# Values of mLSTM and retention as three fp32r products of high and low parts, in a kernel of four layers on one core

## The chip, the cores and the metric

One Trainium2 chip, one core. The metric is the device time of one execution in microseconds (us). The kernel before was timed in three runs; one further execution was profiled.

## The reference, cut to what matters

Two blocks of two layers each, on 256 tokens of 1024 features. The change touches the first block's two mixers and one product of the second block:

```python
rq = _rotary(r_q, pos); rk = _rotary(r_k, pos) * 128 ** -0.5          # 4 heads of 128
scores = einsum('bnihd,bnjhd->bnhij', q, k) * decay                   # retention
o = einsum('bnhij,bnjhe->bnihe', scores, v) + ...                     # v: 4 heads of 256
qk = einsum('bnthd,bnshd->bnhts', q, k) * D                           # mLSTM
num = einsum('bnhts,bnshe->bnthe', qk, v) + ...; den = qk.sum(-1) + ...
tail = cumsum(log_keep, axis=3, reverse=True)                         # second block, stick breaking
```

The kernel computes the two chunks of 128 tokens as one causal product over all 256, so that "scores" is three tiles of 128 x 128 per head (384 columns), and values are the products of these tiles with v, the tile as stationary operand. In mLSTM a column of ones beside v gives den.

## The kernel before, in words

**The main stream.** All weights come in units of four k tiles x 512 columns (1 MB). SyncE issues each unit's DMA into one of three `raw` buffers; ScalarE writes its high part (`wh`, fp32 rounded to fp32r, line 947); VectorE subtracts that from raw and writes the low part (`wl`, line 1372); TensorE takes the units in order out of a ring of four. Every projection is three fp32r products: high x high, low x high, high x low. A group (two units, as a rule) is either row-wise ("tok": the activations are stationary, 512 columns of weights stream, output tokens x features) or column-wise ("col": the weights are stationary, 256 tokens stream, output features x tokens). The groups of a first-block layer are mv0, mv1, gate, mqk0, mqk1, rv0, rv1, rq, rk, ga0, ga1, gb0, gb1, rg0, ... (`B1`); those of a second-block layer are q, k, av, ag, cqk, b, cvg, o0, o1.

**PSUM.** Groups take turns on two pairs of banks (`main`, `freed`); TensorE opens both banks of a pair at the start of a group and waits until they have been read. mqk0 has the pair that mv1 had, with the short gate group between. Four other banks (`aux`) serve the small steps, in the order of `AUX1` and `AUX2`.

**The small steps.** `SIDE1` and `SIDE2` say after which pair of k tiles of which group a step is woven in; there are four such slots a group. The engines' programs each walk the same table. "s h" is a head's mLSTM scores, "v h t" its values for token half t, "tq"/"tk" the transposes of rotated q and k, "rs h" and "rp h" scores and values of retention, "sk" the sums of stick breaking. Scores and values are plain fp32 products, which the trace shows as two passes each. VectorE multiplies the scores with the decay in place (line 1510), then TensorE may run the values (line 663). For retention, q and k come out row-wise; VectorE rotates them (lines 1556 to 1561), TensorE transposes (line 670), ScalarE copies to `rqT` and `rkT` (line 1042). ScalarE copies v out of PSUM (`copy_mv`, line 993, `copy_rv`, line 1036) and with that frees v's banks.

In VectorE's program a group first does the low parts that are due, then its slots, then `evac`, what is to be done with the finished banks; lines of one engine run strictly in this order.

## Time and profile before

| | |
|---|---|
| three runs, median (lowest, highest) | 1176.04 us (1175.67, 1177.94) |
| profiled execution, its own time | 1177.04 us |
| its span | 1175.2 us |
| TensorE busy | 1158.7 us, 99% |
| VectorE busy | 747.7 us, 64% |
| ScalarE busy | 570.4 us, 49% |
| DMA, mean over the span | 180 GB/s |
| granted TensorE clock, mean | 0.995 |

Busy time of TensorE counts each matmul until its modelled end, and a matmul begins while the one ahead drains; so the distance from start to start, not the duration, tells what one costs. The time outside of the span (1177.04 - 1175.2) is launch and end.

### The profile page before, as it was taken

What the parts mean: (1) busy time and instruction counts of PE and PEld (TensorE: products, weight loads), DVE (VectorE), ACT (ScalarE), POOL (GpSimd) and SP (SyncE); (2) the same over time, 40 slices, a digit from 0 to 9 for tenths busy, and PEclk for the clock granted to TensorE, in tenths of its full rate; (3) what the DMA queues carried; (4) which work ended last, traced back from release to release, by engine and by line L of the source; (5) the groups of instructions that cost most, each with busy time, mean ns of one, the idle gap of its engine ahead of it and who ended that gap; (6) DMA issues with size and microseconds to landing.
All of it is one profiled execution on the core that took longest, in us unless ns stands there. A gap on an engine that the chain in (4) does not pass through costs nothing.

```text
span 1175.2 us, 18028 instructions
## 1 busy us (share of the span) xinstructions
PE 1158.7 (99%) x7546; PEld 1042.8 (89%) x7546; DVE 747.7 (64%) x1006; ACT 570.4 (49%) x658; POOL 26.2 (2%) x36
## 2 busy tenths in 40 slices
PE   8999999999999999999999999999999899999997
PEld 6988998998999988998998898899988689978996
DVE  4867557667655546686764667755545667875775
ACT  5563445442544434454544534444432466755664
POOL 0000000001000000000000000000000100000000
PEclk9999999999999999999999999999999999999999
DMA  9664454556666463745446556665566353437330
GB/s 340 224 215 144 144 183 176 182 186 199 225 213 191 165 212 115 250 146 177 160 143 200 169 190 215 223 202 183 183 197 215 125 203 124 141 123 263 113 104 36
DMA packets 129871, 211.45 MB, mean 180 GB/s; under 512 B 6528, under 2 KB 52608, under 8 KB 129664
## 3 DMA queue, kind: packets, MB, share of 16 engines
q1 hardware_dynamic: 128048, 204.02, 52.1%
q0 software_dynamic: 1744, 6.29, 1.9%
q8 instruction: 60, 0.98, 0.3%
q14 instruction: 19, 0.16, 0.0%
HBM read 209.24 MB, written 1.05 MB: 179 GB/s over the span
## 4 chain that ended last, share of the span: by engine, by line
PE 92%; DVE 3%; ACT 3%; issue 1%; DMA 0%; POOL 0%; SPq 0%; DVEq 0%; POOLq 0%; ACTq 0%
PE ps L470 88%; PE ps L663 1%; DVE wl L1372 1%; ACT wh L947 1%; PE ps L698 1%; PE ps L603 1%; ACT sg L1110 0%; DMA rv<-in_w_in 0%; PE ps L801 0%; DVE sg L1652 0%; PE ps L670 0%; PE ps L783 0%; DVE xl L1458 0%; ACT xh L983 0%; DVE X L1631 0%
## 5 line engine op out<-in xcount | busy, mean ns | idle before, releaser
L1372 DVE TENSOR_TENSOR wl<-raw,wh 128x2048 fp32r<-128x2048 f32 (+1 forms) x190 | 424.1, 2238 | 175.6 <-ACT wh L947 175.2
L947 ACT ACTIVATE wh<-raw 128x2048 fp32r<-128x2048 f32 (+1 forms) x190 | 359.9, 1900 | 181.7 <-PE ps L470 166.9
L470 PE MATMUL ps<-xh,wh 128*128 128x256 f32 x1200 | 337.3, 282 | 0.0
L470 PE MATMUL ps<-xl,wh 128*128 128x256 f32 x1200 | 332.3, 277 | 0.0
L470 PE MATMUL ps<-xh,wl 128*128 128x256 f32 x1184 | 328.5, 277 | 0.0
L470 PEld LDWEIGHTS ps<-xh,wh 128*128 128x128 f32 x1200 | 225.9, 188 | 3.2 <-issue 2.4
L470 PEld LDWEIGHTS ps<-xl,wh 128*128 128x128 f32 x1200 | 225.9, 188 | 0.4
L470 PEld LDWEIGHTS ps<-xh,wl 128*128 128x128 f32 x1184 | 222.7, 188 | 0.0
L470 PE MATMUL ps<-wh,xh 128*128 128x512 f32 (+1 forms) x512 | 203.9, 398 | 4.9 <-DVE wl L1372 2.7
L470 PE MATMUL ps<-wl,xh 128*128 128x512 f32 (+1 forms) x512 | 197.3, 385 | 0.0
L470 PE MATMUL ps<-wh,xl 128*128 128x512 f32 (+1 forms) x512 | 197.2, 385 | 0.0
L470 PEld LDWEIGHTS ps<-wh,xh 128*128 128x128 f32 x512 | 96.9, 189 | 26.3 <-DVE wl L1372 4.3
L470 PEld LDWEIGHTS ps<-wh,xl 128*128 128x128 f32 x512 | 96.9, 189 | 19.8
L470 PEld LDWEIGHTS ps<-wl,xh 128*128 128x128 f32 x512 | 97.1, 190 | 17.6
L470 PE MATMUL ps<-wh,hdh 128*128 128x512 f32 x176 | 68.7, 390 | 0.0
L470 PE MATMUL ps<-wl,hdh 128*128 128x512 f32 x176 | 68.5, 389 | 0.0
L470 PE MATMUL ps<-wh,hdl 128*128 128x512 f32 x176 | 68.5, 389 | 0.0
L1102 ACT ACTIVATE tmp<-ps 128x512 f32<-128x512 f32 x18 | 10.8, 598 | 63.5 <-PE ps L470 63.5
L470 PEld LDWEIGHTS ps<-wh,hdl 128*128 128x128 f32 x176 | 33.0, 188 | 6.9
L470 PEld LDWEIGHTS ps<-wl,hdh 128*128 128x128 f32 x176 | 33.0, 188 | 6.8
L470 PEld LDWEIGHTS ps<-wh,hdh 128*128 128x128 f32 x176 | 33.0, 188 | 6.6
L425 POOL TENSOR_TENSOR small<-small,cst 128x1 f32<-128x1 f32 (+1 forms) x18 | 17.9, 992 | 894.9 <-DVE small L1660 392.4
(269 smaller groups left out, 1394.5 us busy)
## 6 DMA issues: line engine op xcount, KB each, us to landing
raw<-in_w_in SPq DMA_DIRECT2D x90, 1024.0 KB, 5.0
raw<-in_w_gate_up SPq DMA_DIRECT2D x88, 512.0 KB, 4.8
raw<-in_w_down SPq DMA_DIRECT2D x20, 1024.0 KB, 5.0
raw<-in_w_out SPq DMA_DIRECT2D x16, 1024.0 KB, 5.0
raw<-in_w_proj_ret SPq DMA_DIRECT2D x8, 1024.0 KB, 4.9
raw<-in_w_proj_mlstm SPq DMA_DIRECT2D x8, 1024.0 KB, 4.9
rows<-in_ln_g POOLq DMA_DIRECT2D x4, 512.0 KB, 4.4
rows<-in_ln_b POOLq DMA_DIRECT2D x4, 512.0 KB, 6.0
```

The lines of the kernel that those rows point to most:

```text
L425: pool.tensor_tensor(o, in_, C("mhalf", 0, n), ALU.pow).then_inc(after, 1)
L470: return pe.matmul(o, a, b, start=start, stop=False, skip_group_check=True)
L603: r = pe.transpose(bank[:, tok_half(g)], src[:, P * (4 * q + g):P * (4 * q + g) + P], ident)
L663: r = pe.matmul(bank[:, 0:257], dd_of(h)[:, o:o + P], mv[:, s, h, 0:257], start=(s == 0), stop=(s == t))
L698: r = pe.transpose(bank[:, S * k2 + P * t:S * k2 + P * t + P], src[:, t, tok_half(k)], ident)
L947: act.activation(stretch(wh, u, 0, m), source(u)[:, 0:m], ACT.Copy).then_inc(s_hi, 1)
L1102: act.activation(a_[:, :], main(name, l)[0][:, :], ACT.Silu).then_inc(freed_by(name, l, 0), 1)
L1372: dve.tensor_tensor(stretch(wl, u, a, nk * n), source(u)[:, a:nk * n], f32(stretch(wh, u, a, nk * n)), ALU.subtract).then_inc(s_lo, 1 if a ...
```

## The change

- Values of mLSTM and retention: v is split into `mvh`/`mvl` and `rvh`/`rvl`, decayed scores into `ddh`/`ddl` and `rdh`/`rdl`, all fp32r; each product becomes three (high x high, low x high, high x low). ScalarE writes the high part of v, VectorE the low part, and it is VectorE that now frees v's banks. Scores themselves stay plain fp32. The ones beside v are two columns of `mvh` (258 columns), written once a layer by VectorE.
- rq and rk are column-wise groups. ScalarE copies each bank with its two partition halves exchanged into `tmp` (`swap`), VectorE multiplies with cos and sin tables of 256 columns each (before: 128 each) and adds. The transposes and their copies are gone, and with them four entries of `AUX1`.
- The stick-breaking sums multiply `below` with 384 columns at once, not 256 and 128.
- The first load of the LRU gate weights `gw` moves from the start of POOL's program to behind the first block's last norm, the second to a later event; `gw` lies in the shared area. New buffers are laid over old areas with pads.

```diff
-for _name, _n in (("ident", 128), ("dec", 1024), ("cc", 128), ("ss", 128), ("negm", 256), ("negs", 384), ("lnc", 384),
+for _name, _n in (("ident", 128), ("dec", 1024), ("cosr", 256), ("sinr", 256), ("negm", 256), ("negs", 384), ("lnc", 384),
...
-    put("cc", lay(np.cos(ang)))
-    put("ss", lay(np.sin(ang)))
+    put("cosr", np.concatenate([np.cos(ang).T, np.cos(ang).T]))
+    put("sinr", np.concatenate([-np.sin(ang).T, np.sin(ang).T]))
...
-            cols(w, c0, 512, SKEW if c0 in (3072, 3584, 6152, 6664, 7176, 7688) else 0)
+            cols(w, c0, 512, SKEW if c0 in (3072, 3584, 0, 512, 6152, 6664, 7176, 7688) else 0)
...
-        "tq0", "tq1", "tk0", "tk1", "rs0", "rs1", "rp0", "rs2", "rp1", "rs3", "rp2", "rp3",
+        "rs0", "rs1", "rp0", "rs2", "rp1", "rs3", "rp2", "rp3",
...
-    "rk": (("v 3 0",), ("v 3 1",), ("hm1", "tq 0"), ("tq 1", "hm2")),
-    "ga0": ((), (), ("tk 0",), ("tk 1",)),
+    "rk": (("v 3 0",), ("v 3 1",), ("hm1",), ("hm2",)),
...
-            pool.dma_start(gw[:, :, :], A["gw"][0:4].rearrange("n p c -> p n c")).then_inc(s_gw, 16)
...
+            pool.wait_ge(s_xn, 16)
+            pool.dma_start(gw[:, :, :], A["gw"][0:4].rearrange("n p c -> p n c")).then_inc(s_gw, 16)
...
-                    r = pe.matmul(bank[:, 0:257], dd_of(h)[:, o:o + P], mv[:, s, h, 0:257], start=(s == 0), stop=(s == t))
-                r.then_inc(fill, 1)
-
-            def ret_turn(l, which, t):
-                bank, fill = open_aux(f"t{which}{t}", l)
-                pe.wait_ge(s_rot, 4 * l + 2 * (which == "k") + t + 1)
-                for h in range(4):
-                    r = pe.transpose(bank[:, tok_half(h)], tmp[3 + t][:, tok_half(h)], ident)
+                    mm(bank[:, 0:258], ddh[:, h, o:o + P], mvh[:, s, h, :], s == 0)
+                    mm(bank[:, 0:258], ddl[:, h, o:o + P], mvh[:, s, h, :], False)
+                    r = mm(bank[:, 0:DV], ddh[:, h, o:o + P], mvl[:, s, h, :], False)
...
-                    aux_done("tk1", l)
+                    pe.wait_ge(s_rot, 4 * l + 4)
...
+                hi, lo, cols = rdh[h % 2], rdl[h % 2], slice(DV * h, DV * h + DV)
                 for t in range(2):
                     for s in range(t + 1):
                         o = P * t if s == 0 else S
-                        r = mm(bank[:, DV * t:DV * t + DV], tmp[3 + h % 2][:, o:o + P], rv[:, s, DV * h:DV * h + DV], t == 0)
+                        out_ = bank[:, DV * t:DV * t + DV]
+                        mm(out_, hi[:, o:o + P], rvh[:, s, cols], t == 0)
+                        mm(out_, lo[:, o:o + P], rvh[:, s, cols], False)
+                        r = mm(out_, hi[:, o:o + P], rvl[:, s, cols], False)
...
-                for name in ("rv0", "rv1", "rq"):
+                for name in ("rv0", "rv1"):
                     one(name, xh, xl, xw, "tok")
-                one("rk", xh, xl, xw, "tok")
-                for name in ("ga0", "ga1", "gb0", "gb1"):
+                for name in ("rq", "rk", "ga0", "ga1", "gb0", "gb1"):
...
-                        mm(bank[:, 0:S], below[:, :], part[:, h, 0:S], part is eeh)
-                        r = mm(bank[:, S:S + P], below[:, :], part[:, h, S:S + P], False)
+                        mm(bank[:, 0:S + P], below[:, :], part[:, h, :], part is eeh)
...
-                act.activation(mv[:, t, 2 * c:2 * c + 2, 0:256], main(f"mv{c}", l)[t][:, :].rearrange("p (h d) -> p h d", h=2),
-                               ACT.Copy).then_inc(freed_by(f"mv{c}", l, t), 1)
+                act.activation(mvh[:, t, 2 * c:2 * c + 2, 0:DV], main(f"mv{c}", l)[t][:, :].rearrange("p (h d) -> p h d", h=2),
+                               ACT.Copy).then_inc(s_mvh, 1)
...
+                    act.activation(rvh[:, t, col_half(c)], main(f"rv{c}", l)[t][:, :], ACT.Copy).then_inc(s_rvh, 1)
+
+            def swap(l, which):
+                main_full("r" + which, l)
+                for b in range(2):
+                    bank = main("r" + which, l)[b]
+                    if which == "k":
+                        act.wait_ge(s_rot, 4 * l + b + 1)
+                    act.activation(tmp[3 + b][0:64, :], bank[64:P, :], ACT.Copy)
+                    act.activation(tmp[3 + b][64:P, :], bank[0:64, :], ACT.Copy).then_inc(s_swap, 1)
...
+            def mv_low(l, t, c):
+                dve.wait_ge(s_mvh, 4 * l + 2 * c + t + 1)
+                cols = slice(2 * c, 2 * c + 2)
+                dve.tensor_tensor(mvl[:, t, cols, :], main(f"mv{c}", l)[t][:, :].rearrange("p (h d) -> p h d", h=2),
+                                  f32(mvh[:, t, cols, 0:DV]), ALU.subtract).then_inc(freed_by(f"mv{c}", l, t), 1)
+
+            def rv_low(l, c):
+                if c == 0:
+                    dve.wait_ge(s_cst, 16)
+                    dve.tensor_scalar(mvh[:, :, :, DV:DV + 2], C("ident", 0, 16).rearrange("p (t h c) -> p t h c", t=2, h=H), 0.0, 1.0, ALU.mult, ALU.add)
+                for t in range(2):
+                    dve.wait_ge(s_rvh, 4 * l + 2 * c + t + 1)
+                    dve.tensor_tensor(rvl[:, t, col_half(c)], main(f"rv{c}", l)[t][:, :], f32(rvh[:, t, col_half(c)]),
+                                      ALU.subtract).then_inc(freed_by(f"rv{c}", l, t), 1)
+
             def ml_scores(l, h):
                 bank, drained = aux_full(f"s{h}", l)
                 dve.wait_ge(s_dec, 4 * l + h + 1)
-                dve.scalar_tensor_tensor(out=dd_of(h), in0=bank[:, 0:384], scalar=128.0 ** -0.5, in1=dd_of(h), op0=ALU.mult,
-                                         op1=ALU.mult).then_inc(drained, 1)
+                dd, hi = dd_of(h), ddh[:, h, 0:384]
+                after(own(dve.scalar_tensor_tensor(out=dd, in0=bank[:, 0:384], scalar=128.0 ** -0.5, in1=dd, op0=ALU.mult, op1=ALU.mult)))
+                after(own(dve.tensor_copy(hi, dd)))
+                dve.tensor_tensor(ddl[:, h, :], dd, f32(hi), ALU.subtract).then_inc(drained, 1)
...
+                name, dst = "r" + which, rqT if which == "q" else rkT
+                cos, sin = (C(n).unsqueeze(1).broadcast_to([P, 2, S]) for n in ("cosr", "sinr"))
+                for b in range(2):
+                    o, other = dst[:, 2 * b:2 * b + 2, :], tmp[3 + b][:, :].rearrange("p (h t) -> p h t", h=2)
+                    dve.wait_ge(s_swap, 4 * l + 2 * (which == "k") + b + 1)
+                    dve.tensor_tensor(o, main(name, l)[b][:, :].rearrange("p (h t) -> p h t", h=2), cos, ALU.mult).then_inc(freed_by(name, l, b), 1)
+                    after(own(dve.tensor_tensor(other, other, sin, ALU.mult)))
+                    main_done(name, l, b)
+                    dve.tensor_tensor(o, o, other, ALU.add).then_inc(s_rot, 1)
 
             def ret_scores(l, h):
                 bank, drained = aux_full(f"rs{h}", l)
-                dd, dec = tmp[3 + h % 2], C("dec", S * h, S * h + S)
+                dd, dec, hi = tmp[3 + h % 2][:, 0:384], C("dec", S * h, S * h + S), rdh[h % 2][:, 0:384]
                 dve.tensor_tensor(dd[:, 0:S], bank[:, 0:S], dec, ALU.mult)
-                dve.tensor_tensor(dd[:, S:S + P], bank[:, S:S + P], dec[:, 0:P], ALU.mult).then_inc(drained, 1)
+                after(own(dve.tensor_tensor(dd[:, S:S + P], bank[:, S:S + P], dec[:, 0:P], ALU.mult)))
+                after(own(dve.tensor_copy(hi, dd)))
+                dve.tensor_tensor(rdl[h % 2][:, 0:384], dd, f32(hi), ALU.subtract).then_inc(drained, 1)
...
-                dve.memset(mv[:, :, :, 256:258], 1.0)
                 if l == 0:
-                    one("mv0", None, 5)
-                    one("mv1")
+                    one("mv0", lambda: [mv_low(l, t, 0) for t in range(2)], 5)
+                    one("mv1", lambda: [mv_low(l, t, 1) for t in range(2)])
                     before_layers()
                 else:
-                    pair(nothing, nothing, l, lambda: split_x("xb", 0, 1, 2), nothing, nothing)
+                    pair(lambda t: mv_low(l, t, 0), lambda t: mv_low(l, t, 1), l, lambda: split_x("xb", 0, 1, 2), nothing, nothing)
```

VectorE's program from the last units of mv0 to the gate of layer 0, before (wl: low part of a unit; the row wh<-raw,wh of 64x8 is the gate's unit; hb and small: small operations for later):

```order
L1372 TENSOR_TENSOR wl<-hret,wh 128x1024
L1372 TENSOR_TENSOR wl<-raw,wh 128x2048 x2
L1370 TENSOR_TENSOR wh<-raw,wh 128x64x8
L1372 TENSOR_TENSOR wl<-raw,wh 128x2048 x2
L1752 TENSOR_SCALAR hb<-par 128x32
```

and now (mvl: low part of v):

```order
L1385 TENSOR_TENSOR wl<-hret,wh 128x1024 x2
L1385 TENSOR_TENSOR wl<-raw,wh 128x2048 x2
L1383 TENSOR_TENSOR wh<-raw,wh 128x64x8
L1523 TENSOR_TENSOR mvl<-ps,mvh 128x512 x2
L1385 TENSOR_TENSOR wl<-raw,wh 128x2048 x2
L1523 TENSOR_TENSOR mvl<-ps,mvh 128x512 x2
L1773 TENSOR_SCALAR hb<-par 128x32
```

The two mvl of mv1 stand behind the low parts of two units, and ahead of the small operations; the two of mv0 stand behind the gate's unit.

VectorE's program around the first mLSTM scores of layer 0, before (hret holds the decayed scores, BN_STATS reads a finished v(h,t)):

```order
L1372 TENSOR_TENSOR wl<-raw,wh 128x2048 x2
L1510 SCALAR_TENSOR_TENSOR hret<-ps,hret 128x384 x2
L1516 BN_STATS small<-ps 128x6
L1372 TENSOR_TENSOR wl<-raw,wh 128x2048
L1516 BN_STATS small<-ps 128x6
```

and now:

```order
L1385 TENSOR_TENSOR wl<-raw,wh 128x2048
L1529 TENSOR_SCALAR mvh<-cst 128x8x2
L1532 TENSOR_TENSOR rvl<-ps,rvh 128x512 x2
L1385 TENSOR_TENSOR wl<-raw,wh 128x2048
L1539 SCALAR_TENSOR_TENSOR hret<-ps,hret 128x384
L1540 CAST ddh<-hret 128x384
L1541 TENSOR_TENSOR ddl<-hret,ddh 128x384
L1539 SCALAR_TENSOR_TENSOR hret<-ps,hret 128x384
L1540 CAST ddh<-hret 128x384
L1541 TENSOR_TENSOR ddl<-hret,ddh 128x384
L1546 BN_STATS small<-ps 128x6
```

Behind each multiplication with the decay there is a cast and a subtraction; the ones and the low part of rv0 come ahead of the low part of a unit that the scores stood behind already.

## Rows read from the trace of the kernel before

**Rows 1.** The page, part 1, TensorE: busy us, share of the span, instructions.

```profile
PE 1158.7 (99%) x7546; PEld 1042.8 (89%) x7546; DVE 747.7 (64%) x1006; ACT 570.4 (49%) x658; POOL 26.2 (2%) x36
```

**Rows 2.** What TensorE waited for: us in total, times, longest us.

```profile
PE ps L603 <- DVE sg L1652: 3.9, 3, 1.7
PE ps L470 <- DVE wl L1372: 2.7, 2, 2.0
```

**Rows 3.** Busy time of each engine in stretches, TensorE clock, DMA share, GB/s.

```profile
core 0: us, PE busy (x) PEld busy (x) DVE busy (x) ACT busy (x) POOL busy (x), PEclk, DMA share, GB/s
223.00:253.00 30.00, 30.00 (x257) 30.00 (x256) 18.70 (x16) 12.88 (x9) 0.00 (x0) 1.00 0.54 176
310.00:340.00 30.00, 30.00 (x267) 30.00 (x266) 16.73 (x13) 14.08 (x13) 0.00 (x0) 1.00 0.66 208
10.70:14.20 3.50, 3.50 (x9) 2.73 (x10) 3.40 (x4) 2.11 (x2) 0.00 (x0) 0.51 1.06 399
928.90:932.40 3.50, 3.46 (x10) 2.58 (x11) 3.35 (x4) 1.16 (x2) 0.57 (x1) 0.51 0.58 131
1044.90:1048.30 3.40, 3.37 (x18) 2.74 (x19) 2.55 (x5) 2.70 (x3) 0.00 (x0) 1.00 0.22 84
```

**Rows 4.** Timeline, TensorE, first v(h,1): start us, us, engine, line, op, out<-in, count.

```profile
82.69 1.03 PE L663 MATMUL ps<-mv,hret 128*128 128x257 f32 x4
...
83.78 0.39 PE L470 MATMUL ps<-wl,xh 128*128 128x512 f32 x1
```

**Rows 5.** Timeline, TensorE, values of retention of the third head, layer 0.

```profile
142.51 1.46 PE L470 MATMUL ps<-rv,tmp 128*128 128x256 f32 x6
...
143.92 0.28 PE L470 MATMUL ps<-xl,wh 128*128 128x256 f32 x1
```

**Rows 6.** Timeline, TensorE, second transposes of q, layer 0.

```profile
111.10 0.60 PE L670 MATMUL ps<-cst,tmp 128*128 128x128 f32 x4
...
111.66 0.29 PE L470 MATMUL ps<-xl,wh 128*128 128x256 f32 x1
```

**Rows 7.** Timeline, TensorE, sums with below, second block, layer 0.

```profile
1015.44 0.39 PE L470 MATMUL ps<-eeh,below 128*128 128x256 f32 x2
1015.67 0.40 PE L470 MATMUL ps<-eel,below 128*128 128x256 f32 x2
```

**Rows 8.** Timeline, ScalarE, end of mv1, layer 0.

```profile
30.19 1.92 ACT L947 ACTIVATE wh<-raw 128x2048 fp32r<-128x2048 f32 x1 [2.32 <-DMA raw<-in_w_in]
32.02 1.06 ACT L993 ACTIVATE mv<-ps 128x512 f32<-128x512 f32 x2
```

**Rows 9.** Timeline, TensorE, first product of mqk0, layer 0.

```profile
33.33 0.28 PE L470 MATMUL ps<-xh,wh 128*128 128x256 f32 x1
```

**Rows 10.** Timeline, VectorE, same place.

```profile
32.22 2.29 DVE L1372 TENSOR_TENSOR wl<-raw,wh 128x2048 fp32r<-128x2048 f32 x1 [1.95 <-ACT wh L947]
34.43 0.17 DVE L1752 TENSOR_SCALAR hb<-par 128x32 f32<-128x32 f32 x1
```

**Rows 11.** Timeline, VectorE, end of rk, layer 0.

```profile
112.02 0.69 DVE L1556 TENSOR_TENSOR tmp<-ps,cst 128x512 f32<-128x512 f32 x1
...
119.33 2.28 DVE L1372 TENSOR_TENSOR wl<-raw,wh 128x2048 fp32r<-128x2048 f32 x1
```

**Rows 12.** Timeline, VectorE, first scores of mLSTM, layer 0.

```profile
76.57 2.29 DVE L1372 TENSOR_TENSOR wl<-raw,wh 128x2048 fp32r<-128x2048 f32 x1 [4.12 <-ACT wh L947]
78.78 1.22 DVE L1510 SCALAR_TENSOR_TENSOR hret<-ps,hret 128x384 f32<-128x384 f32 x2
```

**Rows 13.** Timeline, TensorE, same place.

```profile
78.59 0.81 PE L470 MATMUL ps<-mqk 128*128 128x256 f32 x4
79.43 0.67 PE L663 MATMUL ps<-mv,hret 128*128 128x257 f32 x2
```

**Rows 14.** Instructions by line and form, VectorE: busy us, mean ns, idle before.

```profile
L1510 DVE SCALAR_TENSOR_TENSOR hret<-ps,hret 128x384 f32<-128x384 f32 x8 | 4.5, 556 | 12.0 <-PE ps L470 11.8
...
L1872 DVE CAST eeh<-ee 128x768 fp32r<-128x768 f32 x4 | 2.2, 560 | 0.1
```

**Rows 15.** Timeline, TensorE, first product of the second unit of ga1.

```profile
129.67 0.28 PE L470 MATMUL ps<-xh,wh 128*128 128x256 f32 x1
```

More of the change, by code:

```diff
@@ L239, in program @@
         ls = sb("ls", [P, 8, 4])
-        gw = sb("gw", [P, 4, P])
         areas = ExitStack()
@@ L255, in program @@
             tmp = [a1(f"tmp{i}", [P, 512]) for i in range(5)]
+        with ExitStack() as areas:
+            sb("pad7", [P, 2048], F32, areas)
+            mvh = sb("mvh", [P, 2, H, 258], F32R, areas)
+            sb("pad8", [P, LINE - 16], F32, areas)
+            ddh = sb("ddh", [P, H, 512], F32R, areas)
+            rvh = sb("rvh", [P, 2, D], F32R, areas)
+            sb("pad9", [P, 2048], F32, areas)
+            ddl = sb("ddl", [P, H, 384], F32R, areas)
+            sb("pad10", [P, 512], F32, areas)
+            mvl = sb("mvl", [P, 2, H, DV], F32R, areas)
+            rvl = sb("rvl", [P, 2, D], F32R, areas)
+            rdh = [sb(f"rdh{i}", [P, 512], F32R, areas) for i in range(2)]
+            sb("pad11", [P, 512], F32, areas)
+            rdl = [sb(f"rdl{i}", [P, 512], F32R, areas) for i in range(2)]
         with ExitStack() as areas:
@@ L284, in program @@
         with ExitStack() as areas:
+            sb("pad6", [P, 14848], F32, areas)
+            gw = sb("gw", [P, 4, P], F32, areas)
+        with ExitStack() as areas:
             sb("pad2", [P, 4096], F32, areas)
@@ L453, in gpsimd @@
                 if l == 1:
-                    _, _, drained, n = aux("2l1", 0)
-                    pool.wait_ge(drained, n + 1)
+                    pool.wait_ge(s_yraw, 2)
                     pool.dma_start(gw[:, :, :], A["gw"][4:8].rearrange("n p c -> p n c")).then_inc(s_gw, 16)
@@ L735, in tensor @@
             }
-            steps["tq"] = lambda l, t: ret_turn(l, "q", t)
-            steps["tk"] = lambda l, t: ret_turn(l, "k", t)
             nothing = lambda: None
@@ L1035, in copy_rv @@
                 for t in range(2):
-                    act.activation(rv[:, t, col_half(c)], main(f"rv{c}", l)[t][:, :], ACT.Copy).then_inc(freed_by(f"rv{c}", l, t), 1)
-            def ret_turn(l, which, t):
-                bank, fill, drained, n = aux(f"t{which}{t}", l)
-                act.wait_ge(fill, n + 1)
-                dst = rqT if which == "q" else rkT
-                act.activation(dst[:, :, tok_half(t)], bank[:, :].rearrange("p (h c) -> p h c", h=4), ACT.Copy).then_inc(drained, 1)
+                    act.activation(rvh[:, t, col_half(c)], main(f"rv{c}", l)[t][:, :], ACT.Copy).then_inc(s_rvh, 1)
[7 more added lines that the diff above has]
+                    act.activation(tmp[3 + b][64:P, :], bank[0:64, :], ACT.Copy).then_inc(s_swap, 1)
             def ret_values(l, h):
@@ L1168, in scalar @@
                     one(f"rv{c}", lambda: copy_rv(l, c))
-                one("rq")
-                one("rk")
+                one("rq", lambda: swap(l, "q"))
+                one("rk", lambda: swap(l, "k"))
                 for n, (dst, o0) in enumerate(((ga, 0), (gb, 8))):
@@ L1541, in rotate @@
             def rotate(l, which):
-                name = "r" + which
-                main_full(name, l)
-                for t in range(2):
-                    bank = main(name, l)[t]
-                    if which == "k":
-                        aux_full(f"tq{t}", l)
-                    if t == 1:
-                        dve.wait_ge(s_rot, 4 * l + 2 * (which == "k") + 1)
-                    x_ = bank[:, :].rearrange("p (h c) -> p h c", c=64)
-                    xs = bank[:, :].rearrange("p (h u c) -> p h u c", u=2, c=64)
-                    cc = C("cc", 64 * t, 64 * t + 64).unsqueeze(1).broadcast_to([P, 8, 64])
-                    ss = C("ss", 64 * t, 64 * t + 64).unsqueeze(1).broadcast_to([P, 4, 64])
-                    a4_ = tmp[2][:, :].rearrange("p (h u c) -> p h u c", u=2, c=64)
-                    b4_ = tmp[3 + t][:, :].rearrange("p (h u c) -> p h u c", u=2, c=64)
-                    dve.tensor_tensor(tmp[2][:, :].rearrange("p (h c) -> p h c", c=64), x_, cc, ALU.mult)
-                    dve.tensor_tensor(b4_[:, :, 0, :], xs[:, :, 1, :], ss, ALU.mult)
-                    dve.tensor_tensor(b4_[:, :, 1, :], xs[:, :, 0, :], ss, ALU.mult).then_inc(freed_by(name, l, t), 1)
-                    main_done(name, l, t)
-                    dve.tensor_tensor(b4_[:, :, 0, :], a4_[:, :, 0, :], b4_[:, :, 0, :], ALU.subtract)
-                    dve.tensor_tensor(b4_[:, :, 1, :], a4_[:, :, 1, :], b4_[:, :, 1, :], ALU.add).then_inc(s_rot, 1)
@@ L1790, in vector @@
                 dve.tensor_scalar(g8, main("gate", l)[0][:, 0:S], R("bif", l), None, ALU.add).then_inc(freed_by("gate", l, 0), 1)
-                for name in ("mqk0", "mqk1", "rv0", "rv1"):
+                for name in ("mqk0", "mqk1"):
                     one(name)
+                for c in range(2):
+                    one(f"rv{c}", lambda: rv_low(l, c))
                 one("rq", lambda: rotate(l, "q"))
```

10 lines of the change are left out of this document (5 added, 5 removed).

## The prediction

> **What bounds the kernel now.** I read the page's table first: TensorE is busy for 99% of the span [rows 1]. Busy time alone proves little, since matmuls overlap, so the next view is the list of TensorE's waits: its two longest entries add up to 6.6 us of 1175 [rows 2]. Then the timeline of the engine: products of high and low parts start one behind the other without a hole, and every step that is woven in between pushes the next product back by its own length. So the kernel takes as long as TensorE's instructions take back to back, plus a few waits. A step that leaves TensorE saves its whole length; an instruction on VectorE or ScalarE costs nothing until TensorE stands waiting for it. The profiled execution took 1177.04 us, its span is 1175.2; the median of the runs shown is 1176.04, so I make the sum in differences and take them from the median.
>
> The unit of the argument: a product of 256 columns in fp32r takes 0.113 us from start to start (267 begin in the 30 us from 310 to 340 [rows 3]), one of 512 twice that, 0.227.
>
> **Part 1, values of mLSTM.** Now v(h,1) is two fp32 products of 257 columns, four passes: the stretch starts at 82.69 and the second normal product behind it at 83.78; less one 0.227 us product that is 0.86 us, so 0.215 us a pass [rows 4]. v(h,0) has half. Per head 1.29 us. After: nine fp32r products of 256 to 258 columns, 9 x 0.114 = 1.03 us. Saved 0.26 us a head, 2.1 us for eight heads.
>
> **Part 2, values of retention.** Six passes run from 142.51 to 143.92, less one product: 1.30 us [rows 5]. After: nine products of 256 columns, 1.02 us. Saved 0.28 x 8 = 2.2 us.
>
> **Part 3, the transposes of q and k.** Four transposes run from 111.10 to 111.66, less one product: 0.45 us [rows 6]. Eight such steps go: 3.6 us. The projections rq and rk keep their columns: 12 products of 256 for a k tile in place of 6 of 512, the same 1.36 us.
>
> **Part 4, one product with below.** A pair of 256 and 128 columns takes 1015.67 - 1015.44 = 0.23 us, as long as two of 256 [rows 7]: the 128 columns pay for 256. As one product of 384 columns at the pace of the long ones it is 0.17. Sixteen pairs: 0.9 us saved. The Trainium skill (TensorE: Matmul & The Clock Gate, section Back-to-back issue gap) speaks against this part: it gives a sustained 81 ns for products of 128 columns with their weight loads, by which the pair would cost 0.19 us, the merging would give about 0.4 us, and the sum would be 0.5 us smaller. The trace disagrees for fp32r.
>
> Parts 1 to 4 take 8.8 us off TensorE.
>
> **What comes back: the hand-over of mv1's banks.** This is the term the diff does not show. After mv1 TensorE has only the gate's short products before mqk0 opens the banks of mv1, both halves at once. Now ScalarE alone frees them: copies at 32.02 for 1.06 us, so until 33.08, and mqk0 starts at 33.33 without a hole [rows 8, 9]. After the change the banks are freed by VectorE's mvl, and in VectorE's order the two mvl stand behind the low part of the next unit, which starts at 32.22 because ScalarE's high part waited for its DMA until 30.19, and is through at 34.43, where the next instruction starts [rows 8, 10]. Two reads of 512 from PSUM follow; one takes 0.69 [rows 11] and two overlapped about 1.30. So the banks are free at 35.7 and mqk0 starts at about 35.8: 2.5 us late. The table of constants grows by 256 columns (128 KB) and the first gw load (256 KB) leaves this stretch: 128 KB at the 399 GB/s of a stretch like it [rows 3] is 0.3 us, by which that DMA lands earlier. I take 2.2 us. Bounds: 0.9 if the mvl were free to run directly behind the copies, 2.9 if the longer table delays the DMA and the missing gw gives nothing. In layer 1 the same four instructions stand in a loose stretch of VectorE; I put 0 there, 0.3 at most. mqk0's late start shifts all that follows by the same amount.
>
> **What comes back: the first value step.** The first decayed scores of a layer are made late: VectorE has the low part that starts at 76.57 ahead of them, the scores start at 78.78, and v(0,0) starts at 79.43, though TensorE was through with the scores' four passes (two of 256, two of 128 columns: 3 x 0.215 = 0.65 us from 78.59) at 79.24 [rows 12, 13]. That wait of 0.19 us is there now. After, the bank is released only behind a cast and a subtraction of 384 columns. The subtraction is like the operation of that size, 0.56 us; the cast lies between 0.56 (768 columns, the row) and the 0.17 of the shortest VectorE operations, I take 0.36 [rows 14, 10]; with two waits of VectorE on itself at some 0.04 it is 1.0 us later. Two layers: 2.0 us, bounds 1.4 and 2.4. The other seven heads have a whole slot, 2.7 us of products and more, between scores and values: nothing there.
>
> **What is hidden.** Rotation: VectorE has six operations of 512 columns for ten shorter ones, about the same time; ScalarE has four half-partition copies more for two fewer, 1.2 us more per projection; low parts of rv, four reads of 0.69 a layer; splits of retention scores, 1.0 us a head. The cover is the ring of four units: the low part that starts at 119.33 (the first of two, so done by 121.6) is for the unit that TensorE enters at 129.67 [rows 11, 15]. Eight microseconds of cover, and no stretch here gains more than three on VectorE. Were it gone, each low part would come late by what exceeds it. On POOL the first gw load moves from the start to behind the first block's last norm; behind it there stand the next gain's load and the powers, which wait for later events, and its reader is the LRU step four groups further on.
>
> **The pace.** Column-wise groups run at one of two paces: 257 products in 30 us from 223 to 253, 267 from 310 to 340 [rows 3], 4% apart, and the pace holds until an insertion changes it. rq and rk become column-wise (384 products of 0.113 us in the two layers), and the insertions that change the pace for them and for the four groups behind (768 products) are other ones. At 4.5 ns a product, half of 1152 being slow is 2.6 us; the four groups pay some 0.8 of it now. Bounds -0.8 (all fast) and +4.4 (all slow). The stretch from 223 to 253 lies behind a direct change from row-wise to column-wise (out of mo1 into yr0), as rq now does behind rv1; but fp32 steps remain that can change it, I take +1.2.
>
> Sum: -8.8 + 2.2 + 2.0 + 1.2 = -3.4; 1176.0 - 3.4 = 1172.6 us.
>
> **Rivals.**
> 1. *The clock falls once more.* TensorE's granted clock fell from 2.4 to 1.2 GHz for some 3.5 us from 10.7, behind the wait of 2.0 us, and from 928.9, behind one of 1.7 us; from 1044.9, behind another of 1.7 us, it stayed whole [rows 2, 3]. The new wait of 2.2 us is of that kind. Half clock for 3.4 us costs 1.7 us: 1174.3 us. For it: the wait is longer than all three. Against: products lie directly ahead of it and behind it.
> 2. *No new waits.* VectorE comes to mvl ahead of the low part, or the split is shorter than I think, and TensorE keeps the whole gain: 1176.0 - 8.8 + 1.2 = 1168.4 us. Against it is the order of VectorE's instructions, which is fixed.
> 3. *The slow pace everywhere.* All 1152 products at the slower pace: 3.2 us more, 1175.8 us. For it: direct changes begin slow.
> 4. *Slower than before: splits stand behind the products.* If the split of each head is ready only when its values step has been reached, 14 more steps wait 1.0 us each: 1186.6 us. It decides from the point where bank wait, scores, cast and subtraction, with a low part of 2.3 us ahead of them, exceed the slot of at least 2.7 us plus the steps in it. In a mean slot they make some 4 us against 4.4; for the first step of rv1 alone the order forces it. So little chance.
> 5. *The change does not do what it says:* fp32r products of 258 or 384 columns might cost as much a column as fp32 ones. The 512-column rows are at the fast rate, so I give it 2%; it would be slower too.
>
> **Chances.** A measurement of this kernel tells about 0.2% (2.35 us) from no change. My forecast 0.42, with its own range 1170.6 to 1174.6; rival 1 0.25; rival 2 0.13; rival 3 0.12; rivals 4 and 5 together 0.08. Faster means below 1173.7: four fifths of the forecast, three tenths of rival 1, all of rival 2, which is 0.54. Slower: 0.08. The rest, 0.38, is within 0.2%. The range goes from the lower end of rival 2 to the upper of rivals 1 and 3 together.
>
> **What would show it.** In the profile after: no four-transpose steps behind rq and rk; nine products in about 1.02 us in each of the eight heads' steps, in both parts; single products of 384 columns 0.17 apart; TensorE's list of waits with a new first entry, on VectorE's mvl, once, of 2 us or more, at mqk0 of layer 0; one on ddl at about 1 us, twice; low parts of weights still ready long before their units. The forecast is wrong if the mvl wait is absent or occurs in both layers, if values steps behind the first also wait, or if the stretches with no edit in them differ by more than 1 us.

## The result, and the profile after

| | before | after |
|---|---|---|
| median, us (lowest to highest; runs) | 1175.79 (1174.14 to 1179.48; 22) | 1173.26 (1172.15 to 1177.21; 22) |
| profiled execution, its span | 1177.04, 1175.2 | 1174.51, 1172.7 |

The ratio is 0.9981, 95% interval 0.9974 to 0.9987: the change saves 2.2 us (1.5 to 3.1), with 8.8 us of TensorE work taken away on paper. The two medians are 2.5 us apart. The forecast was 1172.6. The page, part 1, after [rows 1]:

```profile
PE 1151.2 (98%) x7738; PEld 1045.6 (89%) x7738; DVE 769.9 (66%) x1038; ACT 575.5 (49%) x666; POOL 26.1 (2%) x36
```

What TensorE waited for, after (us in total, times, longest) [rows 2]:

```profile
PE ps L618 <- DVE sg L1673: 3.9, 3, 1.7
PE ps L485 <- DVE wl L1385: 3.0, 3, 1.5
PE ps L485 <- DVE mvl L1523: 2.4, 1, 2.4
PE ps L485 <- DVE xl L1471: 2.1, 4, 0.8
PE ps L485 <- issue: 2.0, 2, 1.0
PE ps L485 <- POOL gb L446: 1.1, 1, 1.1
PE ps L485 <- DVE yl L1867: 0.3, 2, 0.2
```

Three entries are new: mvl once, "issue" twice, and 0.3 us on yl. The list has a third wait on wl too, 0.41 us at 928.5, but it is not the change's: VectorE begins that low part 1.34 us behind sg now and 1.33 before, and in the trace of before the clock had fallen just there, so that TensorE came to it later. The first is the hand-over of mv1's banks in layer 0. ScalarE, VectorE and TensorE, after (start, us, engine, line, operation) [rows 8 to 10]:

```profile
29.18 1.93 ACT L957 ACTIVATE wh<-raw 128x2048 fp32r<-128x2048 f32 x1 [0.88 <-DMA raw<-in_w_in]
31.02 1.07 ACT L1003 ACTIVATE mvh<-ps 128x512 fp32r<-128x512 f32 x2
```

```profile
31.22 2.29 DVE L1385 TENSOR_TENSOR wl<-raw,wh 128x2048 fp32r<-128x2048 f32 x1 [0.51 <-ACT wh L957]
33.43 1.28 DVE L1523 TENSOR_TENSOR mvl<-ps,mvh 128x512 fp32r<-128x512 f32 x2
```

```profile
34.81 0.36 PE L485 MATMUL ps<-xh,wh 128*128 128x256 f32 x1 [2.36 <-DVE mvl L1523]
```

The copies of v end at 32.09; mvl stands behind the low part and begins at 33.43; mqk0 starts at 34.81. The second is the first value step; VectorE and TensorE, after [rows 12, 13]:

```profile
79.55 2.29 DVE L1385 TENSOR_TENSOR wl<-raw,wh 128x2048 fp32r<-128x2048 f32 x1 [2.84 <-ACT wh L957]
81.76 0.55 DVE L1539 SCALAR_TENSOR_TENSOR hret<-ps,hret 128x384 f32<-128x384 f32 x1
82.35 0.36 DVE L1540 CAST ddh<-hret 128x384 fp32r<-128x384 f32 x1
82.74 0.56 DVE L1541 TENSOR_TENSOR ddl<-hret,ddh 128x384 fp32r<-128x384 f32 x1
```

```profile
83.40 0.36 PE L485 MATMUL ps<-mvh,ddh 128*128 128x258 f32 x1 [1.02 <-issue]
```

The view calls it "issue", but v(0,0) starts 0.1 us behind the end of the first ddl. Steps and products, after: v(h,1) from 86.57 to 87.28, values of retention from 147.09 to 148.17, and a head's sums with below [rows 4, 5, 7]:

```profile
86.57 0.28 PE L485 MATMUL ps<-mvh,ddh 128*128 128x258 f32 x1
...
87.28 0.28 PE L485 MATMUL ps<-xh,wh 128*128 128x256 f32 x1
...
147.09 0.28 PE L485 MATMUL ps<-rvh,rdh 128*128 128x256 f32 x1
...
148.17 0.28 PE L485 MATMUL ps<-xh,wh 128*128 128x256 f32 x1
...
1012.28 0.34 PE L485 MATMUL ps<-eeh,below 128*128 128x384 f32 x1
1012.46 0.34 PE L485 MATMUL ps<-eel,below 128*128 128x384 f32 x1
1012.64 0.22 PE L485 MATMUL ps<-eeh,ones 128*128 128x128 f32 x1
```

Six products take 0.71 us (four fp32 passes: 0.86), nine take 1.08 (before: 1.30), single products with below are 0.18 apart. The four-transpose steps behind rq and rk are gone. The stretches, after (us, busy time of each engine, clock, DMA share, GB/s) [rows 3]:

```profile
35.40:38.90 3.50, 3.50 (x20) 3.50 (x19) 1.69 (x2) 3.50 (x3) 0.00 (x0) 0.51 0.71 267
926.80:930.30 3.50, 3.04 (x16) 2.28 (x17) 3.50 (x5) 1.20 (x2) 0.54 (x1) 1.00 0.60 165
148.20:164.20 16.00, 16.00 (x139) 16.00 (x138) 11.21 (x23) 7.69 (x8) 1.65 (x1) 1.00 0.59 195
```

and the last stretch before the change, same kernel lines, same length:

```profile
148.10:164.10 16.00, 16.00 (x143) 16.00 (x143) 11.21 (x23) 7.70 (x8) 1.65 (x1) 1.00 0.61 197
```

The clock fell once, for 3.4 us right behind the new wait (first row), and not behind the waits at the start and near 926 (second row), where it had fallen before. The 17 us behind the last rp step run at the slow pace now, 0.2355 us per 512 columns in place of 0.227: 0.6 us in each layer. (Where the text below counts units at a pace, a unit is 512 columns of such products, two of 256; 72 of them lie in these 17 us.)

### The profile page after: what moved, and what is told of

Its sections match the earlier page's. It is cut to its first block, busy times and chain, and to the rows that moved or that the text cites. A ratio compares the mean times of both kernels' runs of the same rounds, so it can differ in the third digit from the quotient of the medians.

```text
span 1172.7 us, 18451 instructions
## 1 busy us (share of the span) xinstructions
PE 1151.2 (98%) x7738; PEld 1045.6 (89%) x7738; DVE 769.9 (66%) x1038; ACT 575.5 (49%) x666; POOL 26.1 (2%) x36
## 3 DMA queue, kind: packets, MB, share of 16 engines
q8 instruction: 62, 1.02, 0.4%
## 4 chain that ended last, share of the span: by engine, by line
PE 87%; DVE 5%; ACT 4%; issue 2%; DMA 1%; SPq 1%; POOL 0%; DVEq 0%; POOLq 0%; ACTq 0%
PE ps L485 85%; DVE wl L1385 2%; DMA raw<-in_w_in 1%; ACT wh L957 1%; PE ps L712 1%; ACT sg L1123 0%; PE ps L618 0%; PE ps L812 0%; ACT L996 0%; DVE sg L1673 0%; SPq L424 0%; ACT L999 0%; ACT ee L1275 0%; PE ps L794 0%; DVE xl L1471 0%
## 5 line engine op out<-in xcount | busy, mean ns | idle before, releaser
L485 PE MATMUL ps<-xh,wh 128*128 128x256 f32 x1328 | 371.9, 281 | 2.4 <-DVE mvl L1523 2.4
L485 PE MATMUL ps<-xl,wh 128*128 128x256 f32 x1328 | 368.8, 278 | 0.0
L485 PE MATMUL ps<-xh,wl 128*128 128x256 f32 x1312 | 365.0, 278 | 0.0
L485 PEld LDWEIGHTS ps<-xh,wh 128*128 128x128 f32 x1328 | 251.0, 189 | 5.5 <-DVE mvl L1523 2.5
L485 PEld LDWEIGHTS ps<-xl,wh 128*128 128x128 f32 x1328 | 250.8, 189 | 0.2
L485 PEld LDWEIGHTS ps<-xh,wl 128*128 128x128 f32 x1312 | 247.4, 189 | 0.0
L485 PE MATMUL ps<-wh,xh 128*128 128x512 f32 (+1 forms) x448 | 174.6, 390 | 5.3 <-DVE wl L1385 3.0
L485 PE MATMUL ps<-wh,xl 128*128 128x512 f32 (+1 forms) x448 | 171.4, 383 | 0.0
L485 PE MATMUL ps<-wl,xh 128*128 128x512 f32 (+1 forms) x448 | 171.2, 382 | 0.0
L485 PEld LDWEIGHTS ps<-wl,xh 128*128 128x128 f32 x448 | 84.3, 188 | 15.1
```

Of the source, the lines that this page charges most:

```text
L485: return pe.matmul(o, a, b, start=start, stop=False, skip_group_check=True)
```

## Experiments

e1 to e6 and e8 start from the changed kernel, e7 from the kernel before; e9 to e12 build on e3. Medians of the kernel before, timed beside them: 1175.9 us (e1 to e4), 1176.1 (e5 to e8), 1175.6 (e9, e10) and 1176.1 (e11, e12). "Less" and "over" are against the changed kernel's 1173.26, unless said otherwise.

**e1, mvl ahead of the low part**

```diff
-                    one("mv1", lambda: [mv_low(l, t, 1) for t in range(2)])
+                    group_early("mv1", lambda: [mv_low(l, t, 1) for t in range(2)])
...
+            def group_early(name, evac):
+                for i in range(2):
+                    take()
+                    lows(high)
+                    highs(use - 1 + RING)
+                    if i == 0:
+                        lows(high)
+                evac()
+                lows(high)
```

> The changed kernel with one thing moved: in layer 0 VectorE does the two mvl of mv1 ahead of the low part of the second unit of mqk0, not behind it. Theory (the 2.36 us wait at mqk0 is the low part of 2.2 us standing ahead of mvl): ScalarE's copies end at 32.1, the second mvl about 0.75 us later, TensorE arrives at 32.45, so the wait falls from 2.36 to 0.4 to 0.5 us and the time by 1.9 us, from 1173.3 to 1171.4 us. The low part then ends at about 35.1, half a microsecond before TensorE enters its unit at 35.7: no new wait. Rival 1 (the hand-over is bound by the weights' DMA, for which ScalarE's high part waits): the wait stays at 1.5 us or more, the time falls by under 0.9 us. Rival 2 (the low part becomes late): the wait on mvl goes but one on wl of 1 us or more appears 2.7 us later; the time falls by under 1 us.

Measured: 1172.36 us (0.9969 of before, 0.9957 to 0.9981), 0.9 less than the change. VectorE and TensorE in e1:

```profile
30.89 1.29 DVE L1533 TENSOR_TENSOR mvl<-ps,mvh 128x512 fp32r<-128x512 f32 x2 [2.22 <-ACT mvh L1003]
32.09 2.28 DVE L1385 TENSOR_TENSOR wl<-raw,wh 128x2048 fp32r<-128x2048 f32 x1
```

```profile
32.28 0.36 PE L485 MATMUL ps<-xh,wh 128*128 128x256 f32 x1
```

mqk0 starts 0.3 us behind the gate's products and no wait on wl follows: the theory's place is right. The time fell by 0.9 us where 1.9 was expected (the interval of some 1.4 us to either side holds both). Two things make the gain smaller than the 2.36 us of one trace. That wait was long in that execution, as e2 shows. And a smaller wait, labelled "issue", is new where rv0 opens the banks of mqk0: 0.34 us at 57.6 in e1, and 0.36 to 0.56 in e3, e9, e10 and e11. VectorE and TensorE in e3:

```profile
55.72 1.65 DVE L1523 SCALAR_TENSOR_TENSOR mqk<-ps,par,mqk 128x253 f32<-128x253 f32 x4
57.47 0.47 PE L485 MATMUL ps<-wh,xh 128*128 128x512 f32 x1 [0.55 <-issue]
```

In these five traces rv0 starts 0.10 us behind the end of the last of these VectorE operations, which read mqk0's banks. TensorE has come earlier by more than VectorE, and the next hand-over is just in time.

**e2, v(0,0) one slot later**

```diff
-    "rv1": ((), ("s 0",), ("s 1", "v 0 0"), ("v 0 1",)),
+    "rv1": ((), ("s 0",), ("s 1",), ("v 0 0", "v 0 1")),
```

> The changed kernel with the step v 0 0 moved one slot later, into the slot of v 0 1, in both layers. Theory (v(0,0) waits 1.02 us for cast and subtraction of the first scores, because these stand behind a low part): both idle stretches of 1.02 us go and nothing takes their place, since the slot gives 2.7 us of products; 1173.3 - 2.0 = 1171.2 us. Rival (what TensorE gains there it loses at the next hand-over, because VectorE and the auxiliary banks come later by a slot): waits of together 1 us or more appear in the following 30 us, the time falls by under 1 us.

Measured: 1171.34 us (0.9956, 0.9944 to 0.9968), 1.9 less; no "issue" entry is left, no other came. It also tells of the first wait. ScalarE and TensorE in e2:

```profile
29.16 1.93 ACT L957 ACTIVATE wh<-raw 128x2048 fp32r<-128x2048 f32 x1 [0.64 <-DMA raw<-in_w_in]
```

```profile
34.78 0.36 PE L485 MATMUL ps<-xh,wh 128*128 128x256 f32 x1 [0.79 <-DVE mvl L1523]
```

mqk0 starts 5.6 us behind the start of that high part, as in the change (29.18, 34.81), and so in all six traces that keep mvl behind the low part (starts of 28.22 to 29.74, mqk0 at 33.84 to 35.35). The high part's start is the landing of a DMA. The wait is the rest: 0.8, 1.0, 1.3, 1.45, 2.4, 2.9 us, mean 1.6, as DMA and TensorE come early or late. In e2 the clock had fallen at the start, from 12.4 for 3.4 us; TensorE arrived at 33.99, not 32.45, and mqk0 started at 34.78, not 34.81: here the half-clock stretch ahead of the hand-over cost nothing.

**e3, both** (the two diffs above)

> The changed kernel with both: mvl of mv1 ahead of the low part in layer 0, and v 0 0 one slot later in both layers. Theory (the two waits are independent): 1173.3 - 1.9 - 2.0 = 1169.4 us. Rival (the waits share their cover: time that VectorE saves at one is missing at the other): 1170.5 us or more. If the clock falls only where TensorE has waited for over 2 us, this kernel should also show fewer half-clock stretches: its mean clock should be 0.998 or more in most runs.

Measured: 1169.20 us (0.9946, 0.9934 to 0.9957), 4.1 less than the change, where 3.9 was expected. In the trace both waits are gone and neither took the other's place; the new one at rv0 (above) stays. The medians alone do not settle it: e1 and e2 add up to 2.8 us, and the interval reaches to the rival's 1170.5. The mean clock was 0.997 to 0.999 in five of six runs, 0.995 in one; in the change's 22 runs 17 reach 0.997, so it does not tell fewer half-clock stretches from chance.

**e4, below in pairs again**

```diff
-                        mm(bank[:, 0:S + P], below[:, :], part[:, h, :], part is eeh)
+                        mm(bank[:, 0:S], below[:, :], part[:, h, 0:S], part is eeh)
+                        r = mm(bank[:, S:S + P], below[:, :], part[:, h, S:S + P], False)
```

> The changed kernel with the product with below cut into 256 and 128 columns again, as before. Theory (128 columns pay for 256): each of 16 pairs takes 0.227 us, the single product 0.17, so sk steps together are 0.9 us longer: 1174.2 us. Rival (a product of 128 columns has its own shorter pitch, 0.081 us as the notes on the chip have it): 0.4 us longer, 1173.7 us. The timeline decides between them, since the medians are hardly finer than the difference.

Measured: 1174.60 us (0.9989, 0.9980 to 0.9999), 1.3 over the change and too wide to decide; its profiled execution has three half-clock stretches, the change's one. The timeline decides: two heads' sums are 0.23 us longer (0.11 a head, eight heads), so 0.9 us of products in all. An estimate from the 81 ns a product of the Trainium skill (TensorE: Matmul & The Clock Gate, section Back-to-back issue gap) gave less than half of that, 0.4; these rows do not bear it out for fp32r. But the next norm of the same layer begins no later for it: e4 is 2.02 us behind the change at 951.8, 2.48 at 1023.0, and 2.01 at 1042.4. The change loses the 0.47 us on yl. TensorE and VectorE, after, and VectorE before:

```profile
1031.50 0.50 PE L485 MATMUL ps<-wh,yh 128*128 128x512 f32 x1 [0.16 <-DVE yl L1867]
```

```profile
1031.02 0.43 DVE L1867 TENSOR_TENSOR yl<-sg,yh 128x256 fp32r<-128x256 f32 x1 [0.48 <-ACT yh L1238]
```

```profile
1033.55 0.43 DVE L1845 TENSOR_TENSOR yl<-sg,yh 128x256 fp32r<-128x256 f32 x1 [0.48 <-ACT yh L1225]
```

yl comes 2.53 us earlier than before, TensorE's stream had come 2.97 us earlier. The product that needs it starts 0.48 us behind yl's start now and did so 0.60 behind it before (at 1034.15): the cover was 0.1 us. The wait is listed with 0.16 us, counted from the modelled end of the product ahead; from start to start that place and the slower product behind it take 0.44 us more than two products of the stream, which is 0.44 of the 0.47. The second layer does the same.

**e5, values of mLSTM plain; e6, values of retention plain**

```diff
-                    mm(bank[:, 0:258], ddh[:, h, o:o + P], mvh[:, s, h, :], s == 0)
-                    mm(bank[:, 0:258], ddl[:, h, o:o + P], mvh[:, s, h, :], False)
-                    r = mm(bank[:, 0:DV], ddh[:, h, o:o + P], mvl[:, s, h, :], False)
+                    r = mm(bank[:, 0:257], ddh[:, h, o:o + P], mvh[:, s, h, 0:257], s == 0)
...
-                        mm(out_, hi[:, o:o + P], rvh[:, s, cols], t == 0)
-                        mm(out_, lo[:, o:o + P], rvh[:, s, cols], False)
-                        r = mm(out_, hi[:, o:o + P], rvl[:, s, cols], False)
+                        r = mm(out_, hi[:, o:o + P], rvh[:, s, cols], t == 0)
```

The first part of the diff is e5 (with `mvh` and `ddh` declared F32), the second e6 (with `rvh` and `rdh` F32).

> The changed kernel with the values products of mLSTM as plain fp32 again: mvh and ddh hold the unrounded fp32 numbers and mvl and ddl are still made, so that every hand-over and every split stays as it is and only TensorE's instructions differ (v(h,0) one and v(h,1) two products of 257 columns in place of three and six). Theory (start to start in the trace, three fp32r products cost less than two fp32 passes): 0.24 us more a head, so 1.9 us more, 1175.2 us, and both waits of the first value steps stay at about 1.0 us. Rival (the products were worth nothing and only the transposes, the pairs and retention gained): within 0.4 us of 1173.3 us.

> The changed kernel with the values products of retention as plain fp32 again (rvh and rdh hold the unrounded numbers, the splits are still made). Per head the step should take 0.23 us more, 1.9 us in all. Theory on the pace (the slow pace of the 144 products behind the last rp step, 0.6 us a layer, is set by the nine fp32r products ahead of it, since before the change the same stretch ran fast behind six fp32 passes): the stretches of some 17 us behind rp 3 come back to 0.227 us per 512 columns, 1.2 us are saved, and the sum is 1173.3 + 1.9 - 1.2 = 1174.0 us. Rival (the pace comes from the new column-wise stretch ahead, rq to ga1): the stretch stays slow, 1175.2 us.

Measured: e5 1177.59 us (1.0011, 1.0002 to 1.0021), 4.3 over the change where 1.9 was expected. The steps are 0.23 us a head longer, as expected (1.8). Most of the rest is pace, which the expectation had left out: behind fp32 v steps the stretch of rk and ga0 and most slots ahead of it are slow, 120 units of 512 columns a layer more than in the change, 2.1 us in all. 18 us of it, in e5, and in the change:

```profile
108.40:126.40 18.00, 18.00 (x155) 18.00 (x154) 16.88 (x34) 9.81 (x14) 1.65 (x1) 1.00 0.39 124
```

```profile
108.40:126.40 18.00, 18.00 (x161) 18.00 (x160) 16.15 (x34) 11.04 (x17) 1.65 (x1) 1.00 0.35 118
```

e6: 1174.88 us (0.9986, 0.9976 to 0.9996), 1.6 over the change, where the theory had 0.7 and the rival 1.9: the median does not decide, and its ten runs had a lower mean clock (0.9964 on average, the change 0.9970). The timeline does: the stretch behind rp 3 is fast again, as the theory had it, and so are the 12 units behind rp 1:

```profile
146.80:162.80 16.00, 16.00 (x143) 16.00 (x142) 11.21 (x23) 7.70 (x8) 1.65 (x1) 1.00 0.59 198
```

**e7, the columns alone, on the kernel before** (of the change's diff the lines on cos and sin, on rq and rk, `swap`, `rotate`, the transposes and `gw`):

```diff
-                for name in ("rv0", "rv1", "rq"):
+                for name in ("rv0", "rv1"):
                     one(name, xh, xl, xw, "tok")
-                one("rk", xh, xl, xw, "tok")
-                for name in ("ga0", "ga1", "gb0", "gb1"):
+                for name in ("rq", "rk", "ga0", "ga1", "gb0", "gb1"):
```

> The kernel before with one part of the change alone: rq and rk as columns with swap and the new rotation, no transposes (and, since the tables of cos and sin grow, gw in the shared area with its later load). Values stay plain fp32, the sums in pairs. Theory: eight steps of 0.45 us go, no new wait appears (no mvl, no split), the pace costs at most 0.5 us: 1175.9 - 3.6 + 0.3 = 1172.6 us, nearly the whole gain of the change from this part alone. Rival (the swap on ScalarE and the hand-over of rq's banks through it cost what the transposes cost): a wait of 0.5 us or more at the opening of rk's successors in each layer, 1174 us or more.

Measured: 1173.86 us (0.9977, 0.9966 to 0.9989), 2.2 saved where 3.3 was expected. No new wait (but for the 0.41 us on wl near 928, as above); but the v steps are fp32 and the same stretch is slow as in e5:

```profile
106.50:124.50 18.00, 18.00 (x155) 18.00 (x154) 16.88 (x34) 9.85 (x13) 1.65 (x1) 1.00 0.39 124
```

In the trace each layer gains 0.95 us from the scores to ga1, 1.8 of transposes less 0.85 of pace. The parts are not additive: behind fp32 v steps the columns run slowly, behind the change's fp32r ones they do not (and e10 below shows that fp32r alone is not the reason).

**e8, the other order of the rp products**

```diff
-                for t in range(2):
+                for t in (1, 0):
...
-                        mm(out_, hi[:, o:o + P], rvh[:, s, cols], t == 0)
+                        mm(out_, hi[:, o:o + P], rvh[:, s, cols], t == 1 and s == 0)
```

> The changed kernel with the two token halves of each rp step in the other order: the six products of the second half first, then the three of the first. The same instructions, the same number. Theory (the pace behind a step is set by how its products fall in with the weight loads, so the order of operands in the last products decides): the pace behind the rp steps changes in at least one of the four places (135 to 148 us and the 17 us behind). Rival (the pace there belongs to the nine products or to the buffers and not to their order): all four places stay at 0.2355 us per 512 columns and no time changes.

Measured: 1172.51 us in its one run, all four places at 0.2355: the rival holds, the order of the products does nothing here.

**e9 and e11, buffers of retention's scores moved by 64 bytes; e10, ddh as well**

```diff
+            sb("pad12", [P, SKEW], F32, areas)
             rdh = [sb(f"rdh{i}", [P, 512], F32R, areas) for i in range(2)]
-            sb("pad11", [P, 512], F32, areas)
+            sb("pad11", [P, 512 - 2 * SKEW], F32, areas)
```

and in e10 also (the places that index `ddh` change with it)

```diff
+            sb("pad13", [P, SKEW], F32, areas)
-            ddh = sb("ddh", [P, H, 512], F32R, areas)
+            ddh = sb("ddh", [P, H * 512 - SKEW], F32R, areas)
```

> The kernel of e3_both with the four buffers of split retention scores moved in SBUF: rdh 16 columns (64 bytes) up, rdl 16 columns down, by pads alone; no instruction is added or taken away. The trace of e8 shows that the order of the rp products does not set the slow pace behind them, the trace of before shows slow and fast in turn with the head, whose scores lie in one of two buffers. Theory (the pace is set by how the addresses of stationary and moving operand lie to each other: the weights of column-wise groups are skewed by the same 16 columns): the four places behind rp steps run at 0.227 in place of 0.2355 us per 512 columns, 108 units in each layer, 1.9 us less in all: 1167.3 us. Rival (it is the number and kind of the products, nine fp32r ones): the pace of all places stays as it is, 1169.2 us.

> The kernel of e9_rd_shifted once more, for its median. Its one trace runs the four places fast and is 2.3 us ahead of e3_both by the end of the first block, but has two half-clock stretches, 3.2 us, where e3 has none. Theory (the clock falls are chance, the pace is a gain in every execution): the median is 1169.2 - 2.3 = 1166.9 us. Rival (the faster pace draws clock falls, or the gain is given back in the second block): 1168.5 us or more.

> As e9_rd_shifted, and the high part of mLSTM's scores, ddh, moved 16 columns up as well. Theory of addresses: the products of the v steps, now 0.12 us apart, come down to 0.114, and the one slow slot of rq runs fast; 0.4 us in each layer beyond e9: 1166.5 us. Rival (addresses do nothing): 1169.2 us as e3. A third case (the shift does harm, since the stretch of 84 units behind the v steps, fast now, turns slow): 1.5 us more than e9.

Measured: e9 1169.50 us in its one run, e11 1166.65 us (0.9925, 0.9913 to 0.9937), 2.6 less than e3. 16 us behind rp 3, in e3 and in e9:

```profile
143.40:159.40 16.00, 16.00 (x138) 16.00 (x137) 11.21 (x23) 7.69 (x8) 1.65 (x1) 1.00 0.60 196
```

```profile
143.40:159.40 16.00, 16.00 (x143) 16.00 (x143) 11.21 (x23) 7.71 (x8) 1.65 (x1) 1.00 0.58 198
```

Same instructions, same order: the pace follows the address. The rp products themselves stand 0.114 us apart now, nine in 1.02 us. In the trace each layer of e9 gains 1.15 us. e10: 1169.06 us (0.9945, 0.9931 to 0.9960), the third case. The retention places stay fast; the 84 units behind the v steps, fast until then, turn slow, and the v products stay 0.12 us apart, where the expectation had 0.114:

```profile
105.00:123.00 18.00, 18.00 (x155) 18.00 (x154) 16.36 (x34) 10.38 (x16) 1.65 (x1) 1.00 0.36 118
```

So 64 bytes between the operands are right at one step and wrong at another; no rule for which was found.

**e12, weights of the two other slow stretches 128 bytes beside the line**

```diff
-            cols(w, c0, 512, SKEW if c0 in (3072, 3584, 0, 512, 6152, 6664, 7176, 7688) else 0)
+            cols(w, c0, 512, 2 * SKEW if c0 in (3072, 3584) else SKEW if c0 in (0, 512, 6152, 6664, 7176, 7688) else 0)
-        for name, skew in (("w_proj_ret", SKEW), ("w_proj_mlstm", SKEW), ("w_out", 0)):
+        for name, skew in (("w_proj_ret", 2 * SKEW), ("w_proj_mlstm", 2 * SKEW), ("w_out", 0)):
```

> The kernel of e11 with the weights of the two other stretches that always run slowly (mqk0 and mqk1, 80 units of 512 columns; yr and ym, some 190 units; in each layer) put 32 columns beside the line, in place of 16. Theory (slow and fast are set by addresses alone, and here by those of the weights against xh and orh): at least one of the stretches changes its pace; if both turn fast, 2.3 us a layer, 1166.9 - 4.6 = 1162.3 us. Rival (the slow pace there comes from the step ahead, the gate's products or the turn from row-wise groups, and stays until something changes it): no stretch changes, 1166.9 us.

Measured: 1168.79 us (0.9940, 0.9927 to 0.9953), 2.1 more than e11. Both stretches changed, to worse: mqk0's units from 0.2355 to 0.240 us, mqk1's last 24, fast until then, to 0.2375, yr's and ym's to 0.2373. The rival, that no stretch changes, is out. What makes them slow at either address stays open.

## Why the prediction was right, point by point

| term, us | forecast | shown |
|---|---|---|
| values of mLSTM | -2.1 | -1.8 |
| values of retention | -2.2 | -1.8 |
| transposes | -3.6 | -3.6 |
| products with below | -0.9 | -0.9 at the products, 0 at the end of each layer (0 in the sum) |
| hand-over of mv1's banks | +2.2 | +2.4 in the profile, mean +1.6 (in the sum) |
| first value step, twice | +2.0 | +2.0 |
| pace | +1.2 | +1.2 |
| sum | -3.4 | -2.4 |

- **The number.** The measured time is 0.7 us above the forecast, the saving 2.2 to 2.5 us and not 3.4. That the time came out closer than the saving is luck: the forecast stood on the median of three runs, 1176.0, and 22 runs gave 1175.8. And the errors partly cancel: parts 1, 2 and 4 brought 1.6 us less than forecast, the hand-over cost 0.6 less.
- **Parts 1 and 2.** 0.23 us a head and not 0.26 or 0.28: the products stand 0.12 us apart, not 0.113 (nine from 147.09 to 148.17). For retention e9 shows that this is the slow pace: with the buffers moved the nine take the forecast 1.02 us. For mLSTM it stays open, as e10's move left them at 0.12.
- **Part 4** is the step that failed. It was costed as time of TensorE and nothing was named that could be late next; yl had 0.1 us of cover, since VectorE is busy from 1008.9 to 1024.9 (before) almost without a hole and yl comes in that order; each of its operations there is 2.5 us earlier now, as TensorE was ahead of the sums, and none is earlier by the shorter sums. The whole 0.9 us came back as a wait.
- **The hand-over** was right in place, cause and size. It was given as one number, though two of its terms, the landing of a DMA and TensorE's arrival, move by 1.5 us between executions: the time of the banks is fixed (5.6 us behind the high part's start), the wait is not. The high part that waits for the DMA began 1.0 us earlier than before in the profile (29.18, 30.19), where 0.3 was expected.
- **The first value step** came out to 0.02 us, cast at 0.36 us included, and the other seven heads do not wait.
- **The pace** summed to the forecast by other parts than it named, which is luck: of rq, rk and ga0 all but 12 units run fast. Against before, 24 units of ga0 and ga1 a layer turned fast; 12 of rq, the 12 behind rp 1 and the 72 behind rp 3 turned slow, 72 more in all, 0.6 us. The mechanism ("an insertion changes it") was half of it: e9 shows that it is the addresses of the insertion's operands.
- **Rival 1** took place in the profiled execution: 35.4 to 38.9 at 0.51 of the clock. Of the six traces with this wait it fell behind the two longest, 2.4 and 2.9 us, and behind none of 0.8 to 1.45. How often it falls there in the 22 runs is not known. Rivals 2 to 5 did not occur; the splits of the other heads were never late.
- **The signs.** The two waits of the first value step are there, under the name "issue" and not ddl. By the forecast's last sign no stretch without an edit was to differ by over 1 us. Two do: TensorE is 1.5 us later from mqk0 to rv0, and 1.1 earlier behind 926. In each one of the two traces has a half-clock stretch; the sign had left the clock out.

## What to carry to other kernels

A product that gets shorter is worth something only where the next thing TensorE needs is not already just in time: name that thing and its slack for every step, the small ones too. When a bank's release moves to another engine, look at what stands ahead of it in that engine's order; moving the two mvl gave back 0.9 us alone (e1) and 2.1 on top of e2, one table entry 1.9. Where products of one kind run at two paces, compare SBUF addresses before counting instructions: the best version, e11, has every part of the change, two waits less and 64 bytes of pad, and takes 1166.65 us, 0.9925 of before.

## What the runs showed of the hardware

- **Paces by address.** Column-wise fp32r products of 256 columns stand 0.1133 or 0.1178 us apart in the first block (0.1193 to 0.1197 in one stretch of the second, after the change from 999 to 1016, and so in all traces). In these traces the pace of a stretch is set at the insertion ahead of it and stays until the next one; it is the same in both layers, and the same in every trace whose edits leave the insertion and the addresses alone. 64 bytes at the insertion's operands turned 108 units a layer fast (e9) or 84 slow (e10), 64 bytes more at the weights made 0.1178 into 0.120 (e12).
- **Half-clock stretches are partly chance.** Over fourteen traces TensorE's granted clock fell from 2.4 to 1.2 GHz, for 3.4 us each time, behind the wait near 11 us in four (1.80 to 2.13 us long; not behind another of 1.88, nor the nine shorter ones), behind the one near 923 in five and near 1040 in three, though these were 1.66 to 1.73 us long in all fourteen. One takes 1.7 us of full-speed work, which in e2 cost nothing. There are none to three in a trace (that at the program's end left out). They make much of the spread between runs: of the change's 22 runs the two at a mean clock of 0.994 took 1176.8 and 1177.2 us, the three at 0.999 and more 1172.2 to 1172.4.
